# Row reciprocals and norm roots brought onto the free axis by transposition: one change to a two-stack hybrid layer kernel

## What is computed

```python
def rmsnorm(x, g):
    y = x32 * lax.rsqrt(jnp.mean(x32 * x32, axis=-1, keepdims=True) + EPS)
    return y.astype(x.dtype) * g

def hybrid_layer(x, ...):                       # first stack, twice
    h = rmsnorm(x, norm_g)
    proj = jnp.einsum("bsd,de->bse", h, w_in)
    ...
    y_c = window_gqa(...) * jax.nn.silu(c_z)    # softmax over keys and a sink, then p @ v
    y_d = neighborhood_attn(...) * jax.nn.silu(d_z)
    ...
    return x + jnp.einsum("bse,ed->bsd", y, w_out)
```

## Time and profile before

| | us |
|---|---|
| median of three runs | 1272.53 (1272.10 to 1272.92) |
| the profiled execution | 1271.64 |
| its span, first to last instruction | 1269.8 |
| PE busy in the span | 1260.5 (99%) |
| DVE busy | 986.7 (78%) |
| ACT busy | 697.5 (55%) |
| POOL busy | 270.0 (21%) |

### The profile page before, as it was taken

The page is one execution under the profiler, slowest core; times in us unless marked ns, Lnnn a source line. Parts: engine busy times, 40 slices in busy tenths (PEclk is TensorE's granted clock), DMA queues, the critical chain, the costliest instruction groups (busy, mean ns, idle before and its releaser), DMA issues.

```text
span 1269.8 us, 21116 instructions
## 1 busy us (share of the span) xinstructions
PE 1260.5 (99%) x7986; PEld 1124.0 (89%) x7986; DVE 986.7 (78%) x1187; ACT 697.5 (55%) x929; POOL 270.0 (21%) x258
## 2 busy tenths in 40 slices
PE   9999999999999999999999999999999999999998
PEld 8998999888888899988888888888889998888886
DVE  6999789898767679868767778767676986877676
ACT  6674567465444586836444455444458673644444
POOL 2763275283000113201000009100011420100000
PEclk9999999999999999999999999999999999999999
DMA  9854654647666554346666655766654535566661
GB/s 281 257 183 166 202 147 150 180 146 222 198 189 187 156 165 144 128 141 185 196 184 185 198 166 176 214 182 190 198 161 138 166 134 150 177 189 197 193 186 52
DMA packets 281359, 224.02 MB, mean 176 GB/s; under 512 B 25996, under 2 KB 264234, under 8 KB 281288
## 3 DMA queue, kind: packets, MB, share of 16 engines
q1 hardware_dynamic: 279144, 220.23, 57.5%
q10 hardware_dynamic: 2032, 2.67, 0.6%
q0 software_dynamic: 112, 0.15, 0.0%
HBM read 221.85 MB, written 3.14 MB: 177 GB/s over the span
## 4 chain that ended last, share of the span: by engine, by line
PE 90%; DVE 6%; ACT 2%; issue 2%; DMA 0%; POOLq 0%; SPq 0%; DVEq 0%; POOL 0%; ACTq 0%
PE wide L1692 26%; PE wide L1695 13%; PE big L1659 9%; PE big L1660 9%; PE big L1661 8%; PE wide L1659 6%; PE wide L1660 6%; PE wide L1661 6%; DVE w_lo L936 2%; PE wide L1811 1%; PE big L1716 1%; PE big L1800 1%; PE big L1786 1%; DVE work L1345 1%; PE wide L1981 1%
## 5 line engine op out<-in xcount | busy, mean ns | idle before, releaser
L936 DVE TENSOR_TENSOR w_lo<-w_raw,w_hi 128x2048 fp32r<-128x2048 f32 x203 | 475.0, 2342 | 94.5 <-ACT w_hi L512 90.2
L512 ACT ACTIVATE w_hi<-w_raw 128x2048 fp32r<-128x2048 f32 x204 | 389.6, 1911 | 165.0 <-PE big L1661 125.2
L1692 PE MATMUL wide<-h_both,w_hi 128*128 128x512 f32 x1408 | 356.7, 393 | 0.0
L1692 PEld LDWEIGHTS wide<-h_both,w_hi 128*128 128x128 f32 x1408 | 254.6, 189 | 48.5 <-DVE h_both L951 2.0
L1659 PE MATMUL wide<-h_both,w_hi 128*128 128x256 f32 x736 | 213.6, 290 | 0.3 <-DVE h_both L951 0.3
L1660 PE MATMUL wide<-h_both,w_hi 128*128 128x256 f32 x736 | 208.1, 283 | 0.0
L1661 PE MATMUL wide<-h_both,w_lo 128*128 128x256 f32 x736 | 208.1, 283 | 0.0
L1695 PEld LDWEIGHTS wide<-h_both,w_lo 128*128 128x128 f32 x1408 | 194.2, 190 | 15.0
L1695 PE MATMUL wide<-h_both,w_lo 128*128 128x256 f32 x1408 | 198.8, 282 | 0.0
L1659 PE MATMUL big<-w_hi,y_hi 128*128 128x512 f32 x480 | 189.1, 394 | 0.0
L1660 PE MATMUL big<-w_lo,y_hi 128*128 128x512 f32 x480 | 187.3, 390 | 0.0
(11 more groups left out here) (254 smaller groups left out, 1459.1 us busy)
## 6 DMA issues: line engine op xcount, KB each, us to landing
w_raw<-in_w_in SPq DMA_DIRECT2D x112, 512.0 KB, 4.7
w_raw<-in_ffn_w_gate SPq DMA_DIRECT2D x88, 512.0 KB, 4.0
w_raw<-in_ffn_w_up SPq DMA_DIRECT2D x88, 512.0 KB, 5.2
w_raw<-in_ffn_w_down SPq DMA_DIRECT2D x88, 512.0 KB, 4.1
w_raw<-in_w_out SPq DMA_DIRECT2D x32, 512.0 KB, 4.3
work<-rpb_shifted SPq DMA_DIRECT2D x32, 64.0 KB, 3.4
rpb_shifted<-rpb_rows SPq DMA_DIRECT2D x10, 147.0 KB
x<-in_x SPq DMA_DIRECT2D x2, 512.0 KB, 6.6
```

The costliest lines, as they stand in the source:

```text
L512: nc.scalar.activation(w_hi[:, r, :], w_raw[:, r, :], ACT.Copy).then_inc(hi_ready, 1)
L936: v.tensor_tensor(w_lo[:, r, :], w_raw[:, r, :], w_hi[:, r, :].bitcast(F32), ALU.subtract).then_inc(lo_ready, 1)
L1692: t_.matmul(o, hi[:, kt, c], h_both[:, kt].rearrange("p a s -> p (a s)"), start=kt == 0, stop=False, skip_group_check=True)
```

## The change

Three edits:

- `spread_rows`: the two products with the identity become two transpositions of the same repeated column.
- `spread_inverse`: the four products become two transpositions of 128 x 128 elements, each for two heads.
- `finish`: in the first stack DVE writes the reciprocals into a new tile `inv_wide`, each repeated 64 times, so that one instruction makes 128 x 256 elements where it made 128 x 4. In both stacks DVE no longer waits for its own reciprocal; the instruction raises `inv_ready` itself.

```diff
+        inv_wide = sb("inv_wide", [P, 2, NH * HD])
...
             def finish(un, u, has_sink):
                 c = 4 * (u % 2)
+                sums = row_sum[:, c:c + 4]
                 dve.wait_ge(probs_exp, un + u + 1)
                 if has_sink:
-                    link(v.tensor_tensor(row_sum[:, c:c + 4], row_sum[:, c:c + 4], sink_e, ALU.add))
-                link(v.reciprocal(row_inv[:, c:c + 4], row_sum[:, c:c + 4]))
-                dve.sem_inc(inv_ready, 1)
+                    link(v.tensor_tensor(sums, sums, sink_e, ALU.add))
+                if un < DEPTH * 4:
+                    pairs = sums.rearrange("p (c low) -> p c low", low=2) if u < 2 else sums.rearrange("p (low c) -> p c low", low=2)
+                    v.reciprocal(inv_wide[:, u % 2, :].rearrange("p (c low d) -> p c low d", c=2, low=2),
+                                 pairs.unsqueeze(3).to_broadcast([P, 2, 2, HD])).then_inc(inv_ready, 1)
+                else:
+                    v.reciprocal(row_inv[:, c:c + 4], sums).then_inc(inv_ready, 1)
...
                 for t in range(NT):
-                    ins = t_.matmul(big[:, 0, t * P:(t + 1) * P], root[:, t:t + 1].to_broadcast([P, P]), ident,
-                                    start=True, stop=True, skip_group_check=True)
+                    ins = t_.transpose(big[:, 0, t * P:(t + 1) * P], root[:, t:t + 1].to_broadcast([P, P]), ident)
                 ins.then_inc(rb_written, 1)
...
-            def spread_inverse(n, u, order=HORDER):
+            def spread_inverse(n, u):
                 pe.wait_ge(inv_ready, n + 1)
                 for c in range(2):
-                    for low in range(2):
-                        at = 4 * (u % 2) + order[2 * c + low]
-                        ins = t_.matmul(aux[low * HD:(low + 1) * HD, c * P:(c + 1) * P],
-                                        row_inv[:, at:at + 1].to_broadcast([P, HD]), ident, start=True, stop=True,
-                                        skip_group_check=True)
+                    ins = t_.transpose(aux[:, c * P:(c + 1) * P], inv_wide[:, u % 2, c * P:(c + 1) * P], ident)
                 ins.then_inc(aux_written, 1)
```

More of the change, by code:

```diff
@@ L1894, in _ @@
                         aux_free()
-                        spread_inverse(l * 4 + u - 2, u - 2, PLAIN if u - 2 < 2 else HORDER)
+                        spread_inverse(l * 4 + u - 2, u - 2)
                 def conv_to_tm():
```

## The result

| | us |
|---|---|
| before, median of five runs | 1272.53 (1271.70 to 1273.19) |
| changed kernel, median of five runs | 1282.53 (1279.73 to 1285.16) |
| ratio | 1.0079, 95% interval 1.0067 to 1.0092 |
| changed kernel, the profiled execution and its span | 1283.38, 1281.6 |

The account below looks back on a forecast made before the run. PE bounds the kernel, but in the first stack's mixers DVE and PE run neck and neck. 4.3 + 3.5 - 1.3 + 2.1 = +8.6 us on the 1272.5 median gives 1281.1; range 1267.8 to 1285.

Parts of the forecast that it names:

- `conv_to_tm` of the first mixer: First mixer: +5.2 on DVE, less the 0.64 wait and 0.22 earlier start, moves PE's conv_to_tm by +4.3 us.
- the second mixer's, the clock aside: Second mixer's conv_to_tm: +5.2 less 1.24 of waits, 0.22 earlier start and 0.27 of POOL's lead, +3.5 us.
- falls of the clock: Behind PE's idle stretch: one fall, in the first mixer, after some 4.5 us idle, +2.1 us; the second left to the range.
- second stack, the clock aside: Second stack: six spread norm roots save 0.22 each, -1.3 us; DVE's dropped wait taken as nothing, up to -0.4.
- price of the reciprocal: DVE, first stack: a 128x256 reciprocal takes 1.77 us, from 4.0 to 6.3 ns per element.
- Rival A: Reciprocal pipelined like any other instruction, 0.44 us, its excess a fixed delay: kernel faster, 1268.5 us; chance 0.20.
- rival D: Reciprocal pays eight steps per element, 2.3 us: 1287.3 us with two falls, 1283.1 if the clock holds; chance 0.15.
- chain of DVE: DVE from unit 0's reciprocal to unit 3's gated_y: longer reciprocals add 5.2 us per mixer, idle only in waits for PE.
- Rival B: Reciprocal at the lower slope, 1.28 us: PE idles 4 us, the clock stays, 1275.1 us; chance 0.15.
- Rival C: The forecast itself, reciprocal 1.6 to 1.9 us: 1279.0 us without a fall, 1283.2 with two; chance 0.45.
- PE's savings: PE's transposed spreads: 1.8 us from norm roots, 3.0 from reciprocals, 4.8 in all; the 1.5 per mixer swallowed.
- The 0.10 that I had given back: Reciprocal spreads of units 2 and 3: saving cut by 0.10, as transpositions lack the value products' 64-wide form ahead.

Follow-up runs that it names:

- sizes: Kernel with transposed norm roots plus, once in the second stack's preamble, trial reciprocals of 128x16 to 128x512 and a 128x256 copy; single run 1283.0 us.
- wide_products: Changed kernel with its wide reciprocals, but inverses spread by four products per unit again, norm roots by transposition; 1278.96 us, ratio 1.0060.
- part_fill: Changed kernel plus 5 unread products of 128x512 in each mixer, ahead of PE's wait at conv_to_tm; 1279.59 us, ratio 1.0064.
- warm: Changed kernel plus 18 unread products of 128x512 in each mixer, ahead of PE's wait at conv_to_tm; 1279.34 us, ratio 1.0050.
- rows_only: Kernel before with only the norm roots spread by transposition; inverses by products and reciprocals 128x4 as before; 1270.49 us, ratio 0.9988.
- copy: Changed kernel with a 128x4 reciprocal that a DVE copy repeats to 128x256, in place of the wide reciprocal; 1272.08 us, ratio 0.9994.
- act_copy: Changed kernel with a 128x4 reciprocal on DVE, without its own wait, repeated to 128x256 by ACT; 1266.97 us, ratio 0.9957.
- unread: Kernel before plus an unread 128x256 reciprocal on DVE ahead of each of the first stack's eight reciprocals; 1287.58 us, ratio 1.0116.
- after_again: The changed kernel itself, unaltered, run and profiled a second time; 1282.34 us, ratio 1.0081.
- unread_half: Kernel before plus an unread 128x128 reciprocal on DVE ahead of each of the first stack's eight reciprocals; 1279.61 us, ratio 1.0060.
- second_only: Changed kernel with wide reciprocals and transposed inverses in the second mixer alone, the first having 128x4 reciprocals and products; 1276.42 us, ratio 1.0037.

## Why the prediction came out as it did

The direction, the mechanism and its place were right: DVE's long reciprocals make POOL's sum late, and PE waits for it in both mixers. The median moved by 10.0 us, where 8.6 was forecast. That it is so near is in part luck: the sum was made for a profiled execution, and the profile's own sum is 11.8 us of span where I had 8.6, and of its four terms two were too low and two too high:

| | forecast | profile |
|---|---|---|
| `conv_to_tm` of the first mixer | +4.3 | +3.84 |
| the second mixer's, the clock aside | +3.5 | +4.3 |
| falls of the clock | +2.1 (one) | +5.3 (two) |
| second stack, the clock aside | -1.3 | -1.7 |

(+4.3 is 231.42 to 242.08, less the 3.84 and the 2.5 of the first fall; -1.7 is 1.14 less 2.8.)

**The price of the reciprocal** was right: 1.77 forecast, 1.75 measured, and 6.25 ns per element at every size where I had worked out 4.0 to 6.3. Rival A, a fixed delay, and rival D, 2.3 us, fall by `sizes`. The Trainium skill ("VectorE: DVE Perf Modes", First, the fixed hardware budget) gives reciprocal a repeat count of 8; the runs show that the iteration is paid per element, at 6.25 ns, not at the eight times 1.04 of rival D.

**The chain of DVE** was right in the first mixer: from unit 0's reciprocal to `gated_y` of unit 3 it takes 36.65 us for 32.11, which with the vanished wait of 0.64 makes 5.18 added, as forecast (5.2). The four reciprocals make 5.12 of that, by the starts of what follows them. From there `conv_to_tm` moved 3.84 and not 4.3, for the 0.45 of the one slow instruction above. The other waits on the way did come, 1.33 us at the values of unit 1, and were taken off the wait at `conv_to_tm` (4.10), as I had said: 5.4 in all for 6.1.

**The second mixer** was mis-sized. There DVE's instructions take 36.93 us for 32.13 less 1.24 of waits: 6.04 added and not 5.2. The reciprocals are the same, 5.13 for the four. The other 0.9 are instructions that take longer when they fall together with POOL's additions. Such slow ones stand in the changed kernel's first mixer too (the cast at 91.61 takes 0.84, the split at 92.95 3.26), but there the kernel before already had as many of them (casts, `y_lo` and splits of 0.73, 0.90, 0.96 and 2.72 between 81 and 95); in its second mixer it lost less to them. My sum let the reciprocals grow and left everything else on DVE as long as it was. Two casts and two splits of the changed kernel, and the POOL rows beside the slower ones:

```profile
212.18 0.29 DVE L944 CAST y_hi<-y_f 128x256 fp32r<-128x256 f32 x1
...
212.97 2.29 DVE L937 TENSOR_TENSOR w_lo<-w_raw,w_hi 128x2048 fp32r<-128x2048 f32 x1
...
220.68 0.85 DVE L944 CAST y_hi<-y_f 128x256 fp32r<-128x256 f32 x1
...
222.02 3.26 DVE L937 TENSOR_TENSOR w_lo<-w_raw,w_hi 128x2048 fp32r<-128x2048 f32 x1
...
219.81 1.56 POOL L1562 TENSOR_TENSOR part_sum<-part_sum,fz 128x256 f32<-128x256 f32 x2 [2.44 <-ACT fz L599]
221.58 1.55 POOL L1581 TENSOR_TENSOR work<-proj 128x512 f32<-128x512 f32 x1 [0.20 <-POOL part_sum L1562]
```

With POOL idle the cast takes 0.29 and the split 2.29. Not every overlap slows: the `y_lo` at 221.56 takes 0.43 beside POOL, where the one at 229.15 takes 0.90. That the overlap is the cause is read from such pairs; no run moved POOL's work.

**The clock** is the step that failed. I took a fall after some 4.5 us of idle time for the rule and counted the first mixer alone, at 2.1 us. It fell in both, 2.6 and 3.2 us into waits of 4.10 and 4.08, and a fall cost 2.5 and 2.8. The 4.5 of the earlier trace rows was one reading of something that varies: at the ends of the programs, where PE does nothing any more, the clock fell 2.4 us (`wide_products`) to 5.3 us (`part_fill`) after PE's last row. Rival B, with four microseconds of idle time and no fall, rested on it too. The 2.1 is also a slip of arithmetic: the four rows start 0.22 apart and make 1.03, so ten would take 2.3 of the 4.25, and the price read there is 1.9. `warm`, `part_fill` and `wide_products` show the sum, 5.3 us, by taking it away. Rival C with two falls, 1283.2, was the closer one.

**PE's savings.** Of the norm roots' 1.8 us `rows_only` shows 1.6. The 3.0 of the reciprocals were 2.5: a spread takes 0.19 to 0.20 from its start to the next product in all four units, where I had 0.14. The 0.10 that I had given back for units 2 and 3 is there, ahead of the spread: 0.20 from the last value product where it was 0.10. It didn't matter, since these savings are swallowed in the mixers, as forecast; not foreseen is that they made things worse by way of the clock. The wait for its own reciprocal that DVE loses in the second stack was taken as nothing. The last column has 1036.72 to 1036.73 in three kernels without it and without a late fall, and 1037.20 in `rows_only`, which has it: about 0.5, a little over the 0.4 that I had kept for it (`copy`, at 1037.05, is 0.4 longer behind PE's last row; up to that row it fits the three). That makes the 1.7 of the table.

On the clock and transpositions: `act_copy`, with all of them, holds 1.00 through both mixers, as `rows_only` does with products for the reciprocals. The Trainium skill ("TensorE: Matmul & The Clock Gate", Part 4: PE-mode transpose) says that they don't count as PE work for the clock. No run here shows a loss from that, and the clock fell in `unread` too, where norm roots and reciprocals are spread by products; a spread of two transpositions is too short a stretch to test it.

## What to carry to other kernels

An operation that costs several times a plain one per element wants its few distinct results computed once and repeated by a copy: here 0.18 us on DVE and 0.41 on ACT in place of 1.75 on DVE. Its cost per element can be had from small instances, by comparing them with a plain operation of the same width. Where two engines run neck and neck, work taken from one by loading the other gains nothing; put the load on a third that idles there (with the copy on ACT the kernel was 1.0043 times faster than before, the dropped wait of DVE included). When one engine shifts against another, look at what now runs side by side: here that moved the end of a mixer by up to 0.9 us. And time saved on an engine ahead of a wait that something else ends is not neutral: the longer idle stretch can bring the clock down behind it.

## What the runs showed of the hardware

- Reciprocal of fp32 on DVE: 0.15 us and 6.25 ns per element and partition from 64 to 512 elements; 0.24 us for 16. A copy of 128 x 256 took 0.29 there (`sizes`).
- What a stay at the lower clock costs goes with its length. Stays of 6.8 us cost 2.5 to 2.8 us (changed kernel twice, `unread` twice, the second mixer of `after_again`), stays of 3.4 us cost 1.5 to 1.6 (first mixer of `after_again`, `unread_half`, `second_only`). The columns give it: for `unread_half` 84.55 less the 82.99 of the kernel before, on which it is built. The same kernel had both: in the first mixer of `after_again` the clock fell only at 114.0, 0.9 us after PE had gone on working, and was back at 117.4, behind the same wait of 4.09.
- When it falls, isn't settled. PE's waits at `conv_to_tm` in the profiled executions and what came: 3.83 to 4.10 us, seven of seven fell (changed kernel twice in each of two profiles, `unread` twice, `second_only` once); 2.87 to 3.11, none of four; 2.26 and 2.27, one of two; 1.70 and 1.72, none of two. Other runs of the kernels with 2.87 to 3.11 did show falls (mean granted clock 0.994 and 0.995 in three). So the length of the wait alone doesn't decide it, and it differed between executions of one program: two of six of `wide_products` show a fall.
- DVE instructions took longer beside POOL's additions: a cast that writes fp32r 0.81 to 0.85 for 0.29, `y_lo` 0.90 for 0.42, a tap 0.84 for 0.49, a split 3.26 for 2.29. Those that read TensorE's results did not (0.41 at 211.27), nor did the reciprocals (1.75 with and without POOL beside them).
